# Order of the hi and the lo product in a wide tile: lo weights first, hi weights second

## The reference

```python
def swiglu(h, w_gate, w_up, w_down):                    # first block, 2 layers, inner width 2816
    return (jax.nn.silu(h @ w_gate) * (h @ w_up)) @ w_down

def swiglu_2(x, w_in, w_out):                           # second block, 2 layers x 2, inner width 4096
    gate, up = jnp.split(x @ w_in, 2, axis=-1)
    return (jax.nn.silu(gate) * up) @ w_out

# hybrid_mixer of the second block: three branches, each with a gate
gates = jax.nn.sigmoid(x @ w_gate + b_gate).reshape(b, t, N_BRANCH, d)
merged = (gates[:, :, 0] * (o_a @ w_br_a) + gates[:, :, 1] * (o_b @ w_br_b)
          + gates[:, :, 2] * (o_c @ w_br_c))
```

## Time and profile before

| | before |
|---|---|
| median of 3 runs | 2266.76 us (2266.72 to 2272.02) |
| the profiled execution, its own time | 2266.66 us |
| its span, first to last instruction | 2264.9 us |
| TensorE matmul busy | 2251.1 us, 15119 matmuls |
| TensorE weight load busy | 2047.7 us |
| VectorE busy | 1781.2 us |
| ScalarE busy | 1285.3 us |
| mean granted TensorE clock | 0.999 |

### The profile page before, as it was taken

The page is one execution under the profiler, slowest core; times in us unless marked ns, Lnnn a source line. Parts: engine busy times, 40 slices in busy tenths (PEclk is TensorE's granted clock), DMA queues, the critical chain, the costliest instruction groups (busy, mean ns, idle before and its releaser), DMA issues.

```text
span 2264.9 us, 37643 instructions
## 1 busy us (share of the span) xinstructions
PE 2251.1 (99%) x15119; PEld 2047.7 (90%) x15119; DVE 1781.2 (79%) x2713; ACT 1285.3 (57%) x2016; POOL 79.4 (4%) x96
## 2 busy tenths in 40 slices
PE   9999999999999999999999999999999999999998
PEld 8988889998888888999999888998889999998887
DVE  7899658879858876897679886698768976798854
ACT  7855455655445555585666554466545856565542
POOL 0022000002100000020000000000000200000000
PEclk9999999999999999999999999999999999999999
DMA  7466565456556665654455555566665543556663
GB/s 244 132 199 196 193 211 176 150 159 215 184 186 214 195 192 191 204 178 129 133 172 193 197 194 190 168 203 206 195 194 197 180 133 122 182 182 221 190 185 100
DMA packets 115084, 412.45 MB, mean 182 GB/s; under 512 B 12896, under 2 KB 14304, under 8 KB 114656
## 3 DMA queue, kind: packets, MB, share of 16 engines
q1 hardware_dynamic: 114480, 407.77, 55.9%
q0 software_dynamic: 288, 2.10, 0.3%
q10 hardware_dynamic: 144, 0.18, 0.0%
HBM read 408.96 MB, written 1.05 MB: 181 GB/s over the span
## 4 chain that ended last, share of the span: by engine, by line
PE 88%; DVE 8%; ACT 2%; issue 1%; DMA 0%; SPq 0%; POOL 0%; DVEq 0%; ACTq 0%
PE ps L452 87%; DVE wlo L2004 3%; DVE region L2796 1%; ACT whi L1244 1%; ACT region L1466 1%; DMA raw<-in_ew_c 0%; PE ps L715 0%; DVE region L2323 0%; DVE RX L2193 0%; DVE x L2051 0%; DVE region L2326 0%; DVE x L2200 0%; DVE region L2439 0%; DVE region L2466 0%; DVE region L2965 0%
## 5 line engine op out<-in xcount | busy, mean ns | idle before, releaser
L452 PE MATMUL ps<-xx,whi 128*128 128x512 f32 (+1 forms) x4504 | 1286.2, 352 | 3.2 <-DVE wlo L2004 2.2
L2004 DVE TENSOR_TENSOR wlo<-raw,whi 128x1024 fp32r<-128x1024 f32 (+3 forms) x772 | 925.2, 1207 | 266.7 <-ACT whi L1244 265.7
L1244 ACT ACTIVATE whi<-raw 128x1024 fp32r<-128x1024 f32 (+3 forms) x772 | 801.1, 1043 | 491.3 <-PE ps L452 481.1
L452 PE MATMUL ps<-xx,wlo 128*128 128x256 f32 x3696 | 1025.0, 277 | 0.0
L452 PEld LDWEIGHTS ps<-xx,whi 128*128 128x128 f32 x4504 | 794.4, 188 | 120.2 <-issue 2.8
L452 PEld LDWEIGHTS ps<-xx,wlo 128*128 128x128 f32 x3696 | 693.8, 188 | 0.4
L452 PE MATMUL ps<-H,whi 128*128 128x512 f32 (+1 forms) x2144 | 571.6, 338 | 0.1
L452 PE MATMUL ps<-H,wlo 128*128 128x256 f32 x1632 | 453.7, 278 | 0.0
L452 PEld LDWEIGHTS ps<-H,whi 128*128 128x128 f32 x2144 | 370.7, 188 | 45.1 <-issue 0.6
L452 PEld LDWEIGHTS ps<-H,wlo 128*128 128x128 f32 x1632 | 306.7, 188 | 0.1
L1999 DVE TENSOR_REDUCE t<-ps 128x256 f32<-128x512 f32 x320 | 219.5, 688 | 31.6 <-PE ps L452 31.2
(11 more groups left out here) (316 smaller groups left out, 1592.4 us busy)
## 6 DMA issues: line engine op xcount, KB each, us to landing
raw<-in_sg SPq DMA_DIRECT2D x128, 512.0 KB, 4.2
raw<-in_su SPq DMA_DIRECT2D x128, 512.0 KB, 4.2
raw<-in_sd SPq DMA_DIRECT2D x128, 512.0 KB, 4.4
raw<-in_mw_g SPq DMA_DIRECT2D x48, 512.0 KB, 3.7
raw<-in_fg SPq DMA_DIRECT2D x44, 512.0 KB, 4.1
raw<-in_fu SPq DMA_DIRECT2D x44, 512.0 KB, 4.2
raw<-in_fd SPq DMA_DIRECT2D x32, 512.0 KB, 3.6
raw<-in_mw_a SPq DMA_DIRECT2D x24, 512.0 KB, 4.2
```

The costliest lines, as they stand in the source:

```text
L452: return e.matmul(out, lhsT, rhs, start=start, stop=stop, skip_group_check=True)
L1244: e.activation(m.whi[:, c % NHL, 0:cw], m.raw[:, c % NRAW, 0:cw], ACT.Copy).then_inc(s["whi"].h, s["whi"].up(c))
L2004: e.tensor_tensor(m.wlo[:, c % NHL, 0:cw], m.raw[:, c % NRAW, 0:cw], m.whi[:, c % NHL, 0:cw].bitcast(F32), ALU.subtract).then_inc(s["wlo"] ...
```

## The change

In `mm2` the two matmuls change places. The l product comes first and carries the start flag of the bank (so at k = 0 it opens the accumulation, writing the left half), and the W product follows, accumulates onto the left half and is the last of the pair. Operands, columns, banks, waits and semaphores stay; the one that raises `gemm` is the last issued, so it is now a W.

```diff
     def mm2(b, wh, wl, a, start):
 
-        mm(b[:, :], wh, a.rearrange("p a b -> p (a b)"), start=start, stop=False)
-        return mm(b[:, 0:256], wl, a[:, 0, :], start=False, stop=True)
+        mm(b[:, 0:256], wl, a[:, 0, :], start=start, stop=False)
+        return mm(b[:, :], wh, a.rearrange("p a b -> p (a b)"), start=False, stop=True)
```

## The result

The changed kernel has a median of 2272.87 us over 20 executions (2267.25 to 2277.65), the kernel before one of 2266.96 us over 20 on the same chip (2266.72 to 2272.36). The ratio is 1.0021, with a 95% interval of 1.0014 to 1.0028: within the 0.3% of "no change", yet clear of zero. By the ratio the time is 2271.7 us, inside the forecast range; the plain median lies 0.9 us above its upper end. A cost of 4 to 6 us where 0 was forecast has to be explained.

What follows compares the result with a forecast made beforehand. TensorE's queue of matmuls was taken to bound the kernel, wide pairs being 1360 us, 60% of the span. The four steps summed to 0 us on 2264.9 of span, giving 2266.8 us, range 2262.8 to 2272.0.

Steps and rivals of the forecast that it cites:

- Step 1: Inside a run of wide pairs: both orders sum to n x 0.340 us, no difference; 1 ns a pair left, 4 us.
- Step 2: At the ends of a run: a first l pays what a first W paid; some 28 runs x 0 = 0.
- Step 3: After the wait for lo weights at 105.4 us: the next product starts at the same time, 0 us.
- Step 4: Behind a chunk's last matmul: `gemm` is raised at the same time, 10 ns less, and its waiters see nothing.
- R1: Slower: W to the next pair's l costs more in each pair, 7 ns x 4000 = 28 us, 2295 us; 6%.
- fewer than 540 pairs in the stretch: Sign of R1 from 1217.2 to 1402 us, where the forecast expected 544 pairs again.
- R2: Faster: W to the next pair's l is shorter, 10 ns x 4000 = 40 us, 2227 us; 3%.
- R3: The start flag opens only the columns its matmul writes: wrong values, no slower, 2266.8 us; under 1%.

Runs made afterwards that it cites:

- e9: Kernel before with the lo product first in the first feed-forward layer alone: all 11 executions at 2266.7 to 2267.0 us, ratio 0.9978.
- e2: Kernel before with the lo product first in the mixers' gate tiles alone: 7 executions at 2267.5 to 2267.6, 4 at 2272.8 to 2272.9 us.
- e5: Kernel before, lo first in the first tile of three long runs behind narrow tiles: 3 executions at 2267.0 to 2267.3, 8 at 2272.1 to 2272.4 us.
- e7: Kernel before, unchanged, run once more for a trace of its upper step: 2272.41 us.
- e8: Kernel before, unchanged, a second execution for a trace of its upper step: 2272.27 us.
- e10: Kernel before, lo first in one gate tile of each of the first block's two feed-forward layers: all 11 executions at 2267.4 to 2267.9 us, ratio 0.9980.
- e11: Kernel before with six more matmuls of 256 columns, one in each feed-forward layer, run for a trace of its upper step: 2273.16 us.
- e12: Kernel before with six more matmuls of 256 columns, as e11, a second execution: 2272.76 us.
- e1: Changed kernel with the old order in the mixers' gate tiles: 4 executions at 2267.0 to 2267.1, 7 at 2271.3 to 2272.6, 1 at 2276.8 us.
- e6: Changed kernel, old order in the gate tiles and the first tile of three long runs behind narrow tiles: all 11 executions at 2267.1 to 2267.6 us.
- e3: Changed kernel with six more matmuls of 256 columns, one in each feed-forward layer: all 11 executions at 2268.5 to 2268.9 us.

## Why the prediction was right or wrong

**What bounds the kernel: right.** In all twelve experiments the traced span differs from that of before by the pairs at 350 ns times 10 ns, within 0.5 us once the extra matmuls (0.7 us) are counted. In the changed kernel the largest sum of waits is 2.2 us, as before, and none grew by more than 0.2.

**Step 1, inside a run: right in what it priced, wrong in its premise.** "A distance depends only on the columns of its first product" is what failed. It depends also on the rhythm that the run is in, 113 + 227 or 117 + 233 ns, and both rhythms occur in both orders. At the same rhythm the order costs nothing, as forecast: 340 ns with l first (1487 to 1671 us) as with W first, and e9 at 2266.8 us with 528 pairs turned round. The bounds of the step, 10 ns more in a pair, happen to be the size of the effect; the 1 ns that I kept for it came from a mean over 544 pairs of one run in one execution, and such a mean says nothing about a second state that this run was not in.

**Step 2, the ends of a run: wrong, and the term that was mis-sized.** I priced an entrance at 0 to 10 ns by its own products. It decides on the pace of all that follows: 5.4 us for 544 pairs. With W first, entrances behind narrow tiles were safe in all 30 cases; with l first 15 of 28 went to 350 ns. The 30 are the long runs; twelve of the 15 are gate runs of 16 pairs. The sum of this term is 0.7 us for the gates (e2) and 0, 4.5, 5.4 or about 10 us for the long runs at 1217, 1481 and 2014 us. The pieces that I did price came out: behind small float32 products a first l takes 204 ns (1110.12 us) where a first W took 317 (1109.94 before), 90 ns over their usual distances both times.

**Step 3, after a wait: right in its arithmetic, blind to the same thing.** The loads are laid as described: lo at 105.49, hi at 105.60 in the changed kernel, and the next l 0.46 us behind the first load, as the next W was before. But this wait was the weak place of the old order. In six traces with the old order there (e5, e7, e8, e10, e11, e12) it is what sets the 350 ns; executions of before stood on that step 9 of 20, 12 of 35, 4 of 21 and 20 of 21 times. The change takes it away: with lo first the stage enters at 350 ns (115, 233, 117 ns at 104.4 us) and the pairs behind the wait were at 340 ns, after three at most, in all five traces, and e9 stood on one step in 11 of 11. So the net is a difference of two: the mean of before lies 2.4 us above its own lowest step (9 of 20 executions at 5.3), which the change gives back, and the mean of the changed kernel lies 5.7 us above its own lowest, for what it loses at three other places; that lowest step is 0.6 us over the one of before. That a sum of 0 came as near as 3.9 us in the mean is in part luck: it left out both sides. How the two balance depends on how often each place is hit: against the 21 executions of e9's chip the changed kernel might have come out level. That was not measured.

**Step 4, what comes behind: right.** The readers of the bank hold nothing up: TensorE's waits are the same to 0.2 us.

**R1** (2295 us) was to show as fewer than 540 pairs in the stretch, and 527 stand there. Its mechanism, another slice for the l, is refuted by the stretch at 1487 us, which has the same slices at 340 ns, and by e7, where the old order runs at 350. A sign named for a rival can come from a cause that nobody listed. **R2** did not occur: no stretch has more than 544 pairs. **R3** concerned values and not time, so none of these times bears on it.

**The range and the chances.** 2262.8 to 2272.0 covers the time by the ratio and misses the plain median by 0.9 us. Its upper end was the highest of three executions of before, 2272.02 us, so that the time by the ratio lies inside owes something to that step, which the sum did not explain. It should have been asked why one of three stood 5.3 us above two that agreed within 0.04. Those 5.3 us over 10 ns are 530 pairs, about one run of wide tiles.

**What stays open.** Why the two rhythms exist, and why a break ends 350 ns in some positions only, the traces don't say. It ended behind W and ahead of l in three cases (the changed kernel, e1, e6) and at two W in a row in one (e10); it did not end behind l and ahead of W in eight (at the product of `rms_stats` in six traces, at the extra one in two), nor at two l in a row (e10). What makes the narrow beat end in one place or another, and the wait at 105.4 us give one rhythm or the other at the same 150 ns, is open too, and so is how e3 lost its steps.

## What to carry to other kernels

Where executions of a kernel stand on steps, take the traces of two steps and compare the mean distance of the same group stretch by stretch before judging any change by its median: here the steps of 5 us were larger than the change of 3.9 us in the mean. Turning the order of the products round cost nothing in each pair here, but it changed which rhythm a long run falls into, and that is read at the entrances of the runs, from the spacing of the products just before them on. Changing the order in one stage only, the one with the weak place (e9), gave 2266.7 to 2267.0 us in all 11 executions, below the mean of both kernels (2269.2 and 2273.1 us, on another chip) and 5.3 us below the median of before beside it.

## What the runs showed of the hardware

A stream of alternating matmuls of 512 and 256 columns, each with its own load of 128 x 128 weights, ran at 340 or at 350 ns a pair, at a granted clock of 0.999 both times. It kept 350 for up to 190 us (543 pairs) and 340 for 378 us (1112 pairs, from 490.7 us in the kernel before) without drifting. With the 256-column product first, 3 to 6 ns between the first two products, and the beat of the narrow products before them, went with one or the other in 28 of 28 entrances. A product of 256 columns set between two tiles ended the longer rhythm where it stood behind a 512-column product (1407.96 us) and left it where it stood ahead of one (e11, e12).

The Trainium skill (TensorE: Matmul & The Clock Gate, Back-to-back issue gap) gives for an isolated matmul at the higher clock its columns over 2.4 GHz plus 2.5 ns, and for a sustained stream of loads and matmuls about 131 ns at 512 columns. By the formula an estimate for such a pair is 216 + 109 = 325 ns. The traces agree with neither: 340 or 350 ns a pair, 227 or 233 of it behind the product of 512 columns.
